# Idle products on TensorE in the state-space heads, and an early load of ScalarE's exponential table

## The chip, the cores and the metric

The kernel runs on one core of a Trainium2 chip. The metric is the device time of one execution in microseconds (us). The engines are TensorE (PE; its weight loads are PEld), VectorE (DVE), ScalarE (ACT), GpSimd (POOL) and SyncE (SP, which here issues DMAs).

## The reference

Two models run one after the other on 512 tokens of width 1024. The second has two layers, and the first layer mixes tokens with a state-space model (Mamba-2 style) of 16 heads, 64 values per head, a state of 128, in 4 chunks of 128 tokens. The part that matters:

```python
cb = jnp.einsum('bclgn,bcsgn->bclsg', cm, bm)
y_diag = jnp.einsum('bclsgr,bcsgrp->bclgrp', cb[..., None] * decay_ls, xdt)
chunk_states = jnp.einsum('bclgn,bclgrp->bcgrpn', bm, xdt * decay_to_end[..., None])
...
_, h_in = lax.scan(step, h0, (chunk_states, chunk_decay))      # h * decay + state, over the chunks
y_off = jnp.einsum('bclgn,bcgrpn->bclgrp', cm, h_in) * jnp.exp(a_cs)[..., None]
y = y_diag + y_off + xs * d_skip
```

`decay_ls` is the exponential of differences of a running sum `a_cs` of one number per head and token; `exp(a_cs)` weights the part that comes from earlier chunks.

## The kernel before

The whole program is one stream of instructions per engine, each executed in its written order, with semaphores between the engines. Almost all of TensorE's time is dense products of width 512 (`product`, L2776). The stretch that the change touches lies between two dense stages of the second model's first layer and takes about 71 us. In it TensorE does, in this order (`second_tensor`):

- **Chunk states** (`chunk_states`, L1931): for each of 3 chunks 2 products of 128x512 in f32. Each chunk waits for its scaled rows (`xde`), which DVE writes at L1642; those of the third chunk reuse the buffer of the first, so DVE waits there for the first chunk's product. DVE then runs the scan over the chunks (L1656 multiplies by the decay, L1660 adds the chunk's product out of PSUM) and raises `hin` at its end.
- **Spreads** (`spread`, L1938): for a head h one f32 product 128x512 that lays the running sum of that head over all partitions, into one of 4 PSUM banks (`aux`). The first four spreads wait for banks that L1660 of the scan gives back.
- **Pairs**: for j = 0 to 7, the spreads of heads 2j+4 and 2j+5 (none for j = 6 and 7), then a wait for DVE (`head_ce`, `head_g`), then the pair's 28 narrow f32 products (L1959, L1961), which multiply the values and the incoming states with the decay matrices of heads 2j and 2j+1 and write the PSUM tile `YD[j % 2]`.

For each head ACT takes the exponential of the spread (`CE`, L1366 or L1369) and of the differences (`GB`, L1367 or L1376); for even heads DVE forms the differences (`head_start`, L1675), for odd heads ACT does (L1372). DVE then multiplies both (`head_end`, L1680 and L1681). `CE` and `GB` have four buffers each, so `head_start(2j+2)` waits until pair j-1 is finished (`yd`). DVE executes `head_start(2j+2)` ahead of `head_end(2j+1)`, on which pair j waits. After `head_end(2j+1)` it adds the skip term to pair j-1 (`head_out`, L1665), which frees `YD` (`yd_taken`).

ACT holds one table of functions at a time. Ahead of the heads it used the table with Silu, so its first exponential (L1366) is preceded by a table load.

`keep_clock(bank, n)` (L2782) issues n f32 products of 128x512 from constants, whose result nobody reads. It is in use at several other places of the kernel.

Of the kernel before, what the change touches and what calls it, by code (L numbers as in the profile page):

```python
# [14 lines left out]
ACT = mybir.ActivationFunctionType  # L15
# [208 lines left out]
GROUP_NO = {g: i for i, g in enumerate(GROUPS)}  # L224
# [94 lines left out]
def build(nc, x_t, params, w_dense, p_t, w_moe, out_t, stop=None):  # L319
    ctx = ExitStack()  # L320
    with ctx:
# [34 lines left out]
        def flat(lo, n):  # L356
            return arena[:, lo:lo + n]
# [30 lines left out]
        def bank(name):  # L388
            return psA[:, AUX_NO[name] % 4, :]
# [4 lines left out]
        def ready(eng, name):  # L394

            eng.wait_ge(sem("aux_ready"), AUX_NO[name] + 1)

        def freed(name):

            return sem(f"aux_free{AUX_NO[name] % 4}")  # L400
# [5 lines left out]
        def group_freed(group):  # L406
            return sem(f"pair_free{GROUP_NO[group] % 2}")
# [835 lines left out]
        CE = [flat(27648 + 512 * i, 512) for i in range(4)]  # L1243
# [3 lines left out]
        ACST, DTT, DEC, DEE = (flat(32768 + 64 * i, 64) for i in range(4))  # L1247
        acst, dtt, dee = (t.rearrange("p (c h) -> p c h", c=4) for t in (ACST, DTT, DEE))
        dec = DEC.rearrange("p (h c) -> p h c", h=16)
        YD = [psD[:, GROUP_NO[("xbc", 5)] % 2, b, :] for b in range(2)]  # L1250
# [28 lines left out]
        def att(i):  # L1279

            n, j = i // 8, i % 8
            return n, j, P if n == 0 else 2 * P
# [31 lines left out]
        def second_act(act, step, root, ahead, x_hi):  # L1314
# [39 lines left out]
            for g in range(2):  # L1354
                n_ = ("stt", 0, g)
                ready(act, n_)
                act.activation(HIN[0][:, 512 * g:512 * g + 512], bank(n_), ACT.Copy).then_inc(freed(n_), 1)
            for h in range(16):
                n_ = ("acs", h)
                ready(act, n_)  # L1360
                if h >= 4:
                    act.wait_ge(sem("yd"), h // 2 - 1)

                if h % 2 == 0:
                    act.wait_ge(sem("seg"), h // 2 + 1)
                    act.activation(CE[h % 4], bank(n_), ACT.Exp).then_inc(freed(n_), 1)  # L1366
                    act.activation(GB[h % 4], GB[h % 4], ACT.Exp).then_inc(sem("seg_exp"), 1)  # L1367
                else:
                    act.activation(CE[h % 4], bank(n_), ACT.Exp)  # L1369
                    for c in range(4):  # L1370
                        cs = slice(P * c, P * c + P)
                        ins = act.activation(GB[h % 4][:, cs], bank(n_)[:, cs], ACT.Relu, bias=acst[:, c, h:h + 1],  # L1372
                                             scale=-1.0)
                    ins.then_inc(freed(n_), 1)
                    act.wait_ge(freed(n_), AUX_NO[n_] // 4 + 1)
                    act.activation(GB[h % 4], GB[h % 4], ACT.Exp, scale=-1.0).then_inc(sem("seg_exp"), 1)  # L1376
                if h == 13:
                    ahead.leave(("z", 0))
# [46 lines left out]
            for layer in range(2):  # L1425
                if layer == 1:
# [4 lines left out]
                    for i in range(N_ATT + 4):  # L1431
                        if i < N_ATT:
                            n, j, w = att(i)
# [13 lines left out]
                        if 2 <= i < N_ATT + 2:  # L1447
                            k = i - 2
                            _, _, w = att(k)
                            n_ = ("pt", k)  # L1450
                            ready(act, n_)
                            if k >= 2:
                                ready(act, ("pv", k - 2))
                            act.activation(PTB[k % 2][:, 0:2 * w], bank(n_)[:, 0:2 * w], ACT.Copy)\
                               .then_inc(freed(n_), 1)
                        if 3 <= i < N_ATT + 3:
                            k = i - 3
                            n, j, _ = att(k)
# [426 lines left out]
                if i >= 1:  # L1885
                    norm(i - 1)

        def second_tensor(pe, aux, filled, dense, colsum, weights, product, tile_of, spread_stat):
            xr = tile_of(X0_P)
            for j in range(8):  # L1890
                dense(("sc_ch", j), xr, at="x0" if j == 0 else None)
# [4 lines left out]
            out = aux(("da_t",))  # L1896
# [10 lines left out]
            for c in range(4):  # L1907
                out = aux(("bct", c))
# [3 lines left out]
            for c in range(4):  # L1912
                for h in range(2):
                    out = aux(("xst", c, h))
# [3 lines left out]
            for g in range(2):  # L1918
                out = aux(("cb", g))
# [8 lines left out]
            def chunk_states(c):  # L1928
                pe.wait_ge(sem("xde"), c + 1)
                for g in range(2):  # L1930
                    filled(pe.matmul(aux(("stt", c, g)), BTOK[:, c, g, :], XDE[c % 2][:, 512 * g:512 * g + 512],  # L1931
                                     start=True, stop=True))

            for c in range(3):
                chunk_states(c)

            def spread(h):
                filled(pe.matmul(aux(("acs", h)), SELH[0:16, h, :], DT[7][0:16, :], start=True, stop=True))  # L1938

            for h in range(4):  # L1940
                spread(h)
            pe.wait_ge(sem("hin"), 1)
            for j in range(8):
                for h in (2 * j + 4, 2 * j + 5):
                    if h < 16:
                        spread(h)
                out = YD[j % 2]
                if j == 0:
                    pe.wait_ge(group_freed(("xbc", 5)), GROUP_NO[("xbc", 5)] // 2 + 1)
                elif j >= 2:  # L1950
                    pe.wait_ge(sem("yd_taken"), j - 1)
                pe.wait_ge(sem("head_ce"), 2 * j + 2)
                pe.wait_ge(sem("head_g"), 2 * j + 2)
                for o_ in range(2):
                    h = 2 * j + o_
                    for c in range(4):
                        cs = slice(P * c, P * c + P)
                        dst = out[HD * o_:HD * o_ + HD, cs]
                        mm = pe.matmul(dst, XDT[:, c, HD * h:HD * h + HD], GB[h % 4][:, cs], start=True, stop=(c == 0))  # L1959
                        if c > 0:  # L1960
                            mm = pe.matmul(dst, HIN[c - 1][:, HD * h:HD * h + HD], CE[h % 4][:, cs],  # L1961
                                           start=False, stop=True)
                mm.then_inc(sem("yd"), 1)
# [58 lines left out]
            for layer in range(2):  # L2022
                if layer == 1:
# [17 lines left out]
                    for i in range(N_ATT + 3):  # L2041
                        if i < N_ATT:
                            n, j, w_ = att(i)
                            k0 = P * n + P - w_
                            out = aux(("sc", i))[:, 0:2 * w_].rearrange("p (o s) -> p o s", o=2)
# [5 lines left out]
                        if 2 <= i < N_ATT + 2:  # L2051
                            k = i - 2
                            _, _, w_ = att(k)
                            out = aux(("pt", k))
                            pe.wait_ge(sem("probs"), k + 1)
                            for b in range(2 * w_ // P):
                                mm = pe.transpose(out[:, P * b:P * b + P], PB[k % 4][:, P * b:P * b + P], ident)
                            filled(mm)
                        if i >= 3:
                            k = i - 3  # L2060
                            n, j, w_ = att(k)
                            nb = w_ // P
                            out = aux(("pv", k))
# [37 lines left out]
        def _(sp_):  # L2101
# [4 lines left out]
            def load(i):  # L2106
                _, nk, nco, _ = PLAN[i]
                if i >= RAW:

                    if i - RAW in SPLIT_NO:  # L2110
                        sp_.wait_ge(sem("w_lo"), SPLIT_NO[i - RAW] + 1)
                    else:
                        sp_.wait_ge(sem("units_done"), i - RAW + 1)
                lo = (i % RAW) * UNIT
                sp_.dma_start(ring[:, lo:lo + nk * nco], w_dense[i, :, 0:nk * nco])\
                   .then_inc(sem(f"ring_full{i % RAW}"), 16)
# [98 lines left out]
        def _(act):  # L2215
# [168 lines left out]
            if stop == 2:  # L2384
                return
            second_act(act, step, root, ahead, x_hi)


# [363 lines left out]
        def _(pe):  # L2752
            done_aux = [0]

            def aux(name):

                n = done_aux[0]
                assert AUX[n] == name, (AUX[n], name)
                done_aux[0] += 1
                if n >= 4:  # L2760
                    pe.wait_ge(sem(f"aux_free{n % 4}"), n // 4)
                return psA[:, n % 4, :]
# [18 lines left out]
            def keep_clock(bank_, n):  # L2781

                for _ in range(n):
                    pe.matmul(bank_, ones, masks[:, 0:SEQ], start=True, stop=True)
# [134 lines left out]
            for o_ in range(2):  # L2919
                out = aux(("lp", o_))  # L2920
# [185 lines left out]
            moe_tensor(pe, aux, filled, dense, colsum, product, keep_clock, spread)  # L3106
            if stop == 2:
                return
            second_tensor(pe, aux, filled, dense, colsum, weights, product, tile_of, spread)

STOP = None

# [27 lines left out]
```

## Time and profile before

| what | value |
|---|---|
| time, median of 3 runs | 2662.4 us (2660.02 to 2664.61) |
| time of the profiled execution | 2666.41 us |
| its span | 2664.7 us |
| mean granted TensorE clock | 0.972 of full speed |
| busy: PE, DVE, ACT, POOL | 95%, 55%, 43%, 6% of the span |

The span is what the profiler recorded of one execution; all times inside the kernel below count from its start. The profiled execution took 4.0 us more than the median of the runs. An f32 product of 128x512 leaves two records on PE, and so two entries in a count such as x12. Records of PE overlap (a product is shown until its result is out), so the distance between the starts of consecutive records tells how long one occupies the engine.

### The profile page before, as it was taken

The page shows a single profiled execution, that of the slowest core. Times are in us where ns is not written, and L with a number is a line of the kernel's source. Part 1 is how long each engine was busy: PE and PEld are TensorE (multiplying, and loading weights), DVE is VectorE, ACT ScalarE, POOL GpSimd, SP SyncE. Part 2 cuts the span into 40 slices and gives each one's busy share as a digit, 9 for nine tenths or more (in the row PEclk, how much of TensorE's full clock was granted, in tenths as well). Part 3 has the DMA queues.
Part 4 walks back from the last instruction along what each step waited for, and adds up shares of the span by engine and source line. Part 5 has one row for each costly group of instructions (what it writes and reads, how often), then busy time and mean ns, then how long its engine had stood idle before and what let it go on. Part 6 is the DMA issues. An engine that isn't in the chain of part 4 may idle for free.

```text
span 2664.7 us, 29458 instructions
## 1 busy us (share of the span) xinstructions
PE 2531.5 (95%) x12112; PEld 1962.4 (74%) x12112; DVE 1477.3 (55%) x1654; ACT 1132.9 (43%) x1329; POOL 147.8 (6%) x168
## 2 busy tenths in 40 slices
PE   7989996999999998999989999999989999999998
PEld 4667864887888886877757768888778567888876
DVE  3675545788888886546565353333454844323334
ACT  3422223777877876322344242122252644212223
POOL 1000001101111100000000100000100010000010
PEclk8888998999999999999979999999999999999999
DMA  6123403899999996322202222232322012232120
GB/s 259 62 72 124 168 10 139 307 369 359 367 352 360 361 357 260 145 96 79 79 1 79 95 71 81 101 109 67 103 77 95 17 48 79 79 108 99 65 101 32
DMA packets 64567, 388.76 MB, mean 146 GB/s; under 512 B 13360, under 2 KB 13488, under 8 KB 22576
## 3 DMA queue, kind: packets, MB, share of 16 engines
q1 hardware_dynamic: 53712, 373.20, 38.3%
q0 software_dynamic: 9280, 8.42, 0.9%
q10 hardware_dynamic: 1440, 5.24, 0.5%
q8 instruction: 97, 1.59, 0.2%
q14 instruction: 38, 0.31, 0.0%
HBM read 391.00 MB, written 20.97 MB: 155 GB/s over the span
## 4 chain that ended last, share of the span: by engine, by line
PE 86%; DVE 6%; ACT 3%; DMA 3%; issue 2%; POOL 0%; SPq 0%; DVEq 0%; ACTq 0%; POOLq 0%
PE psD L2776 71%; DMA ring<-w_moe 1%; PE psA L2015 1%; DMA ring<-w_dense 1%; PE psA L1085 1%; DVE ring_r L2429 1%; PE psA L2849 1%; ACT ring_r L2232 1%; PE psD L1959 1%; PE psA L2976 1%; PE psA L2046 1%; PE psA L3050 1%; PE psA L3036 1%; PE psA L2829 1%; PE psD L1961 1%
## 5 line engine op out<-in xcount | busy, mean ns | idle before, releaser
L2776 PE MATMUL psD<-rounded,ring_r 128*128 128x512 f32 (+1 forms) x6168 | 1457.0, 398 | 16.4 <-DVE ring_r L2429 12.6
L2776 PEld LDWEIGHTS psD<-rounded,ring_r 128*128 128x128 f32 (+1 forms) x6168 | 1159.4, 188 | 314.7 <-issue 23.4
L2429 DVE TENSOR_TENSOR ring_r<-ring,ring_r 128x2048 fp32r<-128x2048 f32 (+3 forms) x143 | 307.1, 2147 | 236.8 <-ACT ring_r L2232 232.6
L2232 ACT ACTIVATE ring_r<-ring 128x2048 fp32r<-128x2048 f32 (+3 forms) x143 | 252.0, 1762 | 390.8 <-PE psD L2776 370.7
L2776 PE MATMUL psD<-ring_r,rounded 128*128 128x512 f32 (+1 forms) x1728 | 410.5, 394 | 5.2 <-DVE rounded L976 2.9
L2776 PEld LDWEIGHTS psD<-ring_r,rounded 128*128 128x128 f32 x1728 | 319.0, 190 | 85.2 <-issue 7.3
L966 DVE TENSOR_TENSOR ring_r<-ring,ring_r 128x2048 fp32r<-128x2048 f32 x128 | 293.2, 2291 | 44.3 <-ACT ring_r L764 41.9
L764 ACT ACTIVATE ring_r<-ring 128x2048 fp32r<-128x2048 f32 x128 | 245.2, 1917 | 53.5 <-PE psD L2776 29.7
L2776 PE MATMUL psD<-rounded,rounded 128*128 128x512 f32 x768 | 191.8, 399 | 0.0
L1792 DVE TENSOR_TENSOR arena<-arena,psD 128x512 f32<-128x512 f32 x44 | 30.3, 688 | 254.7 <-ACT arena L1487 254.7
L2776 PEld LDWEIGHTS psD<-rounded,rounded 128*128 128x128 f32 x768 | 139.7, 188 | 27.1
L966 DVE TENSOR_TENSOR rounded<-ring,rounded 128x2048 fp32r<-128x2048 f32 x64 | 146.5, 2289 | 19.7 <-ACT rounded L764 19.6
L1487 ACT ACTIVATE arena<-psD 128x512 f32<-128x512 f32 x44 | 26.3, 598 | 307.5 <-PE psD L2776 307.4
L764 ACT ACTIVATE rounded<-ring 128x2048 fp32r<-128x2048 f32 x64 | 123.0, 1921 | 8.6 <-DMA ring<-w_moe 8.4
L2238 ACT ACTIVATE rounded<-arena 128x512 fp32r<-128x512 f32 x112 | 67.4, 627 | 59.4 <-DVE arena L1792 36.5
L683 POOL TENSOR_TENSOR arena<-arena 128x512 f32<-128x512 f32 x5 | 7.5, 1505 | 1354.6 <-DVE arena L1765 1280.5
L1765 DVE SCALAR_TENSOR_TENSOR arena<-arena,psD 128x512 f32<-128x512 f32 x40 | 27.5, 688 | 78.0 <-PE psD L2776 77.3
L677 POOL DMA_INDIRECT pair_rows<-arena,ints x32 | 33.9, 1059 | 510.7 <-ACT arena L780 477.4
L1797 DVE TENSOR_TENSOR rounded<-arena,rounded 128x512 fp32r<-128x512 f32 x44 | 30.5, 693 | 30.7 <-ACT rounded L2238 30.7
L971 DVE TENSOR_TENSOR rounded<-psA,rounded 128x1024 fp32r<-128x1024 f32 x32 | 39.2, 1225 | 14.2 <-ACT rounded L769 14.1
L686 POOL TENSOR_TENSOR arena<-arena 128x512 f32<-128x512 f32 x20 | 39.2, 1961 | 97.8 <-DVE arena L1765 92.3
L2849 PE MATMUL psA<-ring,par 128*32 128x256 f32 x384 | 28.7, 426 | 16.2 <-DMA ring<-w_dense 16.2
(423 smaller groups left out, 2094.5 us busy)
## 6 DMA issues: line engine op xcount, KB each, us to landing
ring<-w_moe SPq DMA_DIRECT2D x192, 1024.0 KB, 7.2
ring<-w_dense SPq DMA_DIRECT2D x134, 1024.0 KB, 4.8
ring<-w_dense SPq DMA_DIRECT2D x16, 768.0 KB, 4.1
ring<-w_dense SPq DMA_DIRECT2D x16, 640.0 KB, 3.9
arena<-x_t SPq DMA_DIRECT2D x1, 2048.0 KB, 7.9
token_rows<-arena ACTq DMA_DIRECT2D x4, 512.0 KB, 2.6
arena<-pair_rows SPq DMA_DIRECT2D x4, 512.0 KB, 7.7
arena<-pair_rows ACTq DMA_DIRECT2D x4, 512.0 KB, 8.1
```

The source lines that it names most:

```text
L677: return pool.indirect_dma_start(pair_rows, bass.IndirectOffsetOnAxis(ap=pair_i[:, e:e + 1], axis=0), buf, None, bounds_check=2 * SEQ - 1, ...
L686: step(pool.tensor_tensor(total, total, tiles[k], ALU.add))
L764: act.activation(expert_parts(E.place(j, PARTS))[0], slot_tile(slot), ACT.Copy).then_inc(sem("m_hi"), 1)
L966: dve.tensor_tensor(lo_, slot_tile(E.place(j, RAW)), hi, ALU.subtract).then_inc(sem("m_lo"), 1)
L971: dve.tensor_tensor(XEP[buf][1], x_banks, XEP[buf][0], ALU.subtract).then_inc(sem("xe_lo"), 1)
L1792: dve.tensor_tensor(TH[j % 2], SGT[j % 2], dbank(g)[:, 1, :], ALU.mult)\
L1797: dve.tensor_tensor(HID_P[1][:, j % HS, :], TH[j % 2], HID_P[0][:, j % HS, :], ALU.subtract).then_inc(sem("x_lo"), 1)
L2232: act.activation(parts_of(u, nk, nco)[0], ring_of(u, nk, nco), ACT.Copy).then_inc(sem("w_hi"), 1)
L2238: act.activation(dst, src, ACT.Identity if kw else ACT.Copy, **kw).then_inc(sem("x_hi"), 1)
L2429: dve.tensor_tensor(lo_, ring_of(u, nk, nco), hi, ALU.subtract).then_inc(sem("w_lo"), 1)
L2776: mm = pe.matmul(out, w[a], x[b], start=start and i == 0, stop=stop_ and i == 2)
L2849: mm = pe.matmul(out[32 * (k % 4):32 * (k % 4) + 32, 0:256], par[:, at + k:at + k + 32], w[:, k, :], start=(k < 4), stop=(k >= 4))
```

## The change

Three kinds of instructions are added, and one wait stands earlier; nothing is removed.

```diff
@@ second_act: ahead of the loop over the 16 heads
                 act.activation(HIN[0][:, 512 * g:512 * g + 512], bank(n_), ACT.Copy).then_inc(freed(n_), 1)
+            step(act.activation(CE[3][:, 0:1], DTT[:, 0:1], ACT.Exp))
             for h in range(16):
@@ second_tensor
+            pe.wait_ge(group_freed(("xbc", 5)), GROUP_NO[("xbc", 5)] // 2 + 1)
+            keep_clock(YD[0], 10)
             for c in range(3):
                 chunk_states(c)
...
             for h in range(4):
                 spread(h)
+            keep_clock(YD[0], 6)
             pe.wait_ge(sem("hin"), 1)
             for j in range(8):
                 for h in (2 * j + 4, 2 * j + 5):
                     if h < 16:
                         spread(h)
                 out = YD[j % 2]
-                if j == 0:
-                    pe.wait_ge(group_freed(("xbc", 5)), GROUP_NO[("xbc", 5)] // 2 + 1)
-                elif j >= 2:
+                if j >= 2:
                     pe.wait_ge(sem("yd_taken"), j - 1)
+                keep_clock(out, 5)
                 pe.wait_ge(sem("head_ce"), 2 * j + 2)
                 pe.wait_ge(sem("head_g"), 2 * j + 2)
```

On TensorE, from the chunk states to the second pair, the stream before was this (L1931 is the chunk states, L1938 the spreads, L1959 and L1961 the pairs):

```order
L1922 MATMUL psA<-arena 128x128 x8
L1931 MATMUL psA<-arena 128x512 x6
L1938 MATMUL psA<-arena 128x512 x6
L1959 MATMUL psD<-arena 64x128 x2
L1961 MATMUL psD<-arena 64x128
L1959 MATMUL psD<-arena 64x128
```

And it is now this, with the lines of the changed kernel (L1932, L1941, L1962 and L1964 are the same four, L2787 is `keep_clock`):

```order
L1923 MATMUL psA<-arena 128x128 x8
L2787 MATMUL psD<-masks 128x512 x10
L1932 MATMUL psA<-arena 128x512 x6
L1941 MATMUL psA<-arena 128x512 x4
L2787 MATMUL psD<-masks 128x512 x6
L1941 MATMUL psA<-arena 128x512 x2
L2787 MATMUL psD<-masks 128x512 x5
L1962 MATMUL psD<-arena 64x128 x2
L1964 MATMUL psD<-arena 64x128
```

Ten idle products stand ahead of the chunk states, six behind the first four spreads, and five between the spreads of heads 4 and 5 and pair 0. The same five stand ahead of each later pair; where a pair has no spreads, as the last one, they stand directly between two pairs:

```order
L1962 MATMUL psD<-arena 64x128
L1964 MATMUL psD<-arena 64x128
L2787 MATMUL psD<-masks 128x512 x5
L1962 MATMUL psD<-arena 64x128 x2
L1964 MATMUL psD<-arena 64x128
```

That makes 10 + 6 + 8 x 5 = 56 idle products more. On ACT, between the copies of the first states (L1357) and the first head, before:

```order
L1357 ACTIVATE arena<-psA 128x512 x2
L1366 ACT_TABLE_LOAD
L1366 ACTIVATE arena<-psA 128x512
L1367 ACTIVATE arena<-arena 128x512
```

And now:

```order
L1357 ACTIVATE arena<-psA 128x512 x2
L1358 ACT_TABLE_LOAD
L1358 ACTIVATE arena<-arena 128x1
L1367 ACTIVATE arena<-psA 128x512
L1368 ACTIVATE arena<-arena 128x512
```

The table load moved from the first head's exponential to the new exponential of a single column, which waits for nothing of the heads. DVE's stream and the DMAs are as before.

## Rows read from the trace of the kernel before

**Rows 1.** The page's busy times, one line: engines, busy us, share, instructions.

```profile
PE 2531.5 (95%) x12112; PEld 1962.4 (74%) x12112; DVE 1477.3 (55%) x1654; ACT 1132.9 (43%) x1329; POOL 147.8 (6%) x168
```

**Rows 2.** Windows of PE over the stretch: length, busy, granted clock, DMA share, GB/s.

```profile
1324.83:1396.10 71.27, 58.76 (x269) 0.76 0.00 1
1354.50:1361.80 7.30, 6.37 (x32) 0.77 0.00 0
1383.60:1389.30 5.70, 2.87 (x29) 1.00 0.00 0
1389.30:1396.10 6.80, 6.79 (x56) 0.75 0.01 2
```

**Rows 3.** Windows of PE, cut where the granted clock changes.

```profile
1324.80:1328.00 3.20, 0.06 (x2) 1.00 0.00 0
1328.50:1331.50 3.00, 3.00 (x5) 0.50 0.00 0
1332.00:1338.50 6.50, 6.17 (x15) 1.00 0.00 0
1339.00:1351.90 12.90, 11.03 (x35) 0.50 0.00 0
1352.20:1355.40 3.20, 2.52 (x12) 1.00 0.00 0
1355.70:1359.00 3.30, 3.30 (x21) 0.50 0.00 0
```

**Rows 4.** Timeline, chunk states to pair 0: start, us, engine, line, operation, idle before.

```profile
1327.97 7.09 PE L1931 MATMUL psA<-arena 128*128 128x512 f32 x12 [3.14 <-DVE arena L1642]
...
1331.48 1.23 DVE L1642 TENSOR_TENSOR arena<-arena 128x1024 f32<-128x1024 f32 x1 [2.62 <-PE psA L1931]
...
1332.63 0.68 DVE L1656 TENSOR_TENSOR arena<-arena 128x512 f32<-128x512 f32 x1
...
1337.68 0.69 DVE L1660 TENSOR_TENSOR arena<-arena,psA 128x512 f32<-128x512 f32 x1
...
1338.42 2.02 PE L1938 MATMUL psA<-arena 16*128 16x512 f32 x2 [0.33 <-DVE arena L1660]
...
1339.96 1.28 ACT L1366 ACT_TABLE_LOAD   x1 [7.88 <-DVE arena L1675]
1341.26 0.60 ACT L1366 ACTIVATE arena<-psA 128x512 f32<-128x512 f32 x1
...
1346.32 1.08 PE L1959 MATMUL psD<-arena 128*64 128x128 f32 x4 [0.31 <-DVE arena L1681]
```

**Rows 5.** Timeline of pairs 5 and 6, same columns.

```profile
1380.70 1.98 PE L1938 MATMUL psA<-arena 16*128 16x512 f32 x4
1380.89 1.36 DVE L1675 TENSOR_SCALAR arena<-psA,arena 128x128 f32<-128x128 f32 x4 [2.69 <-PE psD L1961]
...
1383.60 0.62 PE L1959 MATMUL psD<-arena 128*64 128x128 f32 x4 [0.92 <-DVE arena L1681]
...
1386.57 1.37 DVE L1675 TENSOR_SCALAR arena<-psA,arena 128x128 f32<-128x128 f32 x4 [1.26 <-PE psD L1961]
...
1389.29 0.69 PE L1959 MATMUL psD<-arena 128*64 128x128 f32 x4 [2.83 <-DVE arena L1681]
```

**Rows 6.** PE's waits from 1324 to 1397: us in total, times, longest.

```profile
PE psD L1959 <- DVE arena L1681: 7.5, 7, 2.8
PE psA L1931 <- DVE arena L1642: 3.1, 1, 3.1
```

**Rows 7.** Timeline: idle products that the kernel already has (two records per product).

```profile
1063.67 4.46 PE L2784 MATMUL psA<-masks 128*128 128x512 f32 x10
...
1396.93 2.84 PE L2784 MATMUL psD<-masks 128*128 128x512 f32 x6 [0.84 <-DVE arena L1665]
```

**Rows 8.** Timeline of PE alone, from the stretch's end on.

```profile
1399.82 45.03 PE L2776 MATMUL psD<-rounded,ring_r 128*128 128x512 f32 x192
1444.69 7.03 PE L2829 MATMUL psA<-arena,masks 128*128 128x512 f32 x16
1451.16 78.97 PE L2776 MATMUL psD<-rounded,ring_r 128*128 128x512 f32 x336
```

More of the change, by code:

```diff
@@ L1886, in attention, with second_tensor @@
                     norm(i - 1)
-        def second_tensor(pe, aux, filled, dense, colsum, weights, product, tile_of, spread_stat):
+        def second_tensor(pe, aux, filled, dense, colsum, weights, product, tile_of, spread_stat, keep_clock):
             xr = tile_of(X0_P)
@@ L3108, in _ @@
                 return
-            second_tensor(pe, aux, filled, dense, colsum, weights, product, tile_of, spread)
+            second_tensor(pe, aux, filled, dense, colsum, weights, product, tile_of, spread, keep_clock)
 STOP = None
```

## The prediction

> **What bounds the kernel now.** I read the page first: PE is busy 95% of the span [rows 1], so whatever is added to its stream must find a hole there. The windows show that the touched stretch is not like the rest: of 71.3 us PE is busy 58.8, and the granted clock averages 0.76, which means that it runs for about half of the time at 1.2 GHz instead of 2.4 [rows 2]. So there are 12.5 us of idle time and some lost clock to be had. Windows cut at the changes of the clock show when it falls: after PE has been idle for 3 us ahead of the chunk states, again after the first spreads, and in the middle of a pair; each short fall lasts some 3.3 us [rows 3].
>
> The timeline then shows the loop over the pairs [rows 5]. PE issues the two spreads of pair 5 from 1380.70 (1.98 us with the tail of the last record), and pair 5 itself starts at 1383.60, 0.92 us after PE ran out of work, released by DVE's L1681. DVE could start its own work for the next pair (L1675) only at 1380.89, when the pair before was done, and starts the next at 1386.57, when pair 5 is done. So the loop is a ring of two parts: a pair on PE, 1386.57 - 1383.60 = 2.97 us at the full clock, and then 1389.29 - 1386.57 = 2.72 us of DVE and ACT, of which PE fills 1.7 us with spreads where there are any. The table of waits says the same: the pairs waited 7.5 us in 7 waits for L1681, and the chunk states 3.1 us for L1642 [rows 6]. From 1346.32 to 1389.29 six pairs took 42.97 us [rows 4, 5], 7.16 us each, against 2.97 + 2.72 = 5.69 at a full clock: the slow clock costs 1.47 us a pair, the idle time about 1 us.
>
> Behind the stretch PE runs dense products without a gap for well over 100 us [rows 8], so nothing there gives back what the stretch loses, and nothing there was waiting for it to end early.
>
> **What one idle product costs.** Ten records, five products, took 4.46 us [rows 7]. The last record ends some 0.59 us after its start, so the other nine stand 0.43 us apart, and one product holds PE for 0.86 us at the full clock. At half the clock it is double, 1.72: the four records of the chunk states from 1327.97 to 1331.48 are two products of the same shape in 3.5 us [rows 4]. The engine executes in order, so none of this overlaps with the pair behind it. All 56 products cost 56 x 0.86 = 48.2 us of PE. The hole they stand in is 12.5 us, and a perfect clock could return less than half of the time spent at 1.2 GHz. That alone says that the change is too large for its place; the new timeline gives the amount.
>
> **The new timeline, step by step**, with everything at the full clock at first.
>
> - The chunk states. PE is done with the products before them at 1324.85. Ten idle products, 8.6 us, end at 1333.45, where before there was a wait until 1327.97; the clock should stay up, since the idle time that stood ahead of its fall is filled [rows 3]. Six products of chunk states take 5.16 us, to 1338.6.
> - The scan. DVE's third block of scaled rows waits for the first chunk's product, which is ready 1.72 us plus about 0.25 after 1333.45, at 1335.45, instead of 1331.48 [rows 4]. The whole chain of DVE behind it moves by 3.97 us. Its last L1660 started at 1337.68 and now starts at 1341.65 and ends near 1342.4.
> - The first spreads. They wait for banks that this chain frees; the fourth starts at 1342.4 and ends at 1343.25. Six idle products, 5.16 us, end at 1348.4.
> - The clock, once. Before, spreads held apart by DVE's bank returns were followed by a fall of the clock (6.50 us at 1.00, then 0.50) [rows 3]. That phase comes back unchanged in kind, so I take one fall of 3.4 us, the length that the short falls have, through dense work: + 1.7 us, to 1350.1.
> - Pair 0. Two spreads (1.72) and five idle products (4.3) end at 1356.1. ACT and DVE are ready long before: their L1366 started 2.9 us after the scan (with the table load in between) and pair 0 5.06 us after that [rows 4]; with the scan ending at 1342.4 this is 1349 even before anything is gained on ACT. Pair 0 ends at 1356.1 + 2.97 = 1359.1.
> - The table load. It leaves the path between DVE's L1675 and the first exponential, which is worth 1.28 us [rows 4], but that path now ends 7 us ahead of PE. I cost it at nothing. If the idle products were not there it would be worth its 1.28. The single-column exponential costs a fraction of the 0.60 us that a full one takes, in a place where ACT waited 7.88 us [rows 4].
> - Pairs 1 to 5. Spreads start 0.19 us ahead of DVE's L1675 [rows 5], take 1.72, then 4.3 of idle products, then 2.97 of the pair: 8.8 us, with 0.05 for the semaphores 8.85. DVE and ACT need only 2.72 of it behind a pair, so they drop out of the bound. Five pairs: 44.25 us, to 1403.4.
> - Pairs 6 and 7 have no spreads: 4.3 + 2.97 - 0.19 = 7.1 us each, to 1417.6. Pair 7 hurts most: before, it followed pair 6 without any wait, and both took 6.8 us together [rows 2].
> - The end. The next product of PE waited for L1665 of the last pair, some 0.8 us. It started at 1396.93 [rows 7] and now starts at 1418.4: **21.5 us later**.
>
> Against the profiled execution's own span this gives 2664.7 + 21.5 = 2686.2 us and 2687.9 us for its time; against the median of 2662.4, from which that execution stands 4.0 us off, **2683.9 us**. The same by budget: 48.2 of products, less the 12.5 idle, less 14 for the pairs and chunk states that run at the full clock, leaves 21.7.
>
> Of the clock the Trainium skill (TensorE: Matmul & The Clock Gate, "Why this matters for your kernels") says that it falls when long idle gaps stand between bursts of products. Here it fell behind spreads with only sub-microsecond gaps, and within a pair that came after 0.9 us of idle time, so the trace does not bear the rule out as a condition. By the page the fall behind the first spreads would not return, and the sum would be 1.7 us less: 2682.2.
>
> **The rivals.**
>
> - *The clock does not hold.* The pairs are narrow products and the spreads use 16 of the rows, so it may be that neither counts as much activity, and the clock still falls once a pair, for 3.3 us as in [rows 3]. Each fall in a stretch without idle time costs 1.7 us. Seven falls: + 12, so 2696. For it speaks that the clock fell in a pair after spreads that filled most of the time before. Against it: half of every new period consists of full-size products, and such products, back to back, keep the clock at 1.00 elsewhere. That would be "the change does not do what it says". Chance 0.11.
> - *Faster.* If the idle products fitted into the waits, the gain would be: six pairs at 5.69 instead of 7.16, 8.8 us; pairs 6 and 7, 1.0; the table load, 1.28; the first chunk's two products at the full clock, 1.7. Together 12.8 us, 2649.6. The mechanism is real, its size is the question: behind a pair PE has 0.19 + 2.72 = 2.91 us, less 1.72 for spreads, so 1.19 us are free, which is 1.4 products. Each further one adds 0.86 to the pair. It pays up to (1.19 + 1.47) / 0.86 = 3.1 products a pair; the change has 5, plus 16 in front. It could only win if a product took under 0.53 us here, and no row has one of this shape and type at less than 0.86. Chance 0.03. The skill's page ScalarE: Activation LUTs ("What ACT_TABLE_LOAD costs") gives 2.66 us for a switch with its drain, by which this rival would end at 2648.2; here only the 1.28 us of the load stand between L1675 and the exponential.
> - *No change that can be told* (a measurement of this kernel tells 0.2%, 5.3 us, from none). This needs 16 us of the 21.5 to be returned, for instance by dense stages that become shorter since ACT and DVE got ahead in splitting weights. But the splits stand at fixed places of their streams and PE does not wait for them behind the stretch [rows 8]. Chance 0.03.
> - *Slower by less*, 2669 to 2679: products overlap in part with the spreads' tails, or the profiled stretch was worse than that of a usual run. Chance 0.08.
>
> **How the numbers follow.** The forecast, 2684 with 2679 to 2689 of its own (with or without the one fall, 0.1 us either way a pair, 2 us of spread between runs), has 0.75. To leave out no more than 2 in 10 I widen it upward by the lesser half of the first rival: **2678 to 2692**. Slower by over 0.2%: 0.75 + 0.11 + 0.08 = 0.94; within 0.03; faster 0.03.
>
> **What would show the steps.** In the new trace idle products should fill 8.6 us ahead of the chunk states; the starts of the pairs should stand 8.85 us apart for pairs 1 to 5 and 7.1 behind; PE's wait for L1681 should be gone and DVE should wait 3 us more a pair for PE; the clock of the stretch should be near 1.00 except for one fall of 3.4 us near 1342 to 1346; the table load should stand near 1335; the stretch should be 93 us long instead of 71.3. A stretch at a mean clock of 0.8 would mean the first rival. I am wrong altogether if an idle product occupies PE for clearly less than 0.86 us, or if a dense stage behind gets shorter.

## The result, and the profile after

The changed kernel takes 2690.1 us in the median of 4 runs (2683.8 to 2692.7), against 2663.5 for before. The ratio is 1.0097, with a 95% interval of 1.0083 to 1.011: slower by about 26 us. The forecast was 2684 with 2678 to 2692.

The profiled execution of the changed kernel is the fastest of the four, 2683.8 us with a span of 2682.0. At least part of what it is ahead by has nothing to do with the change: the stretch began 6.5 us earlier in it than in the profile of before. The page's busy times, against [rows 1], show 34 us more of PE, with the 112 records of the 56 products, and next to nothing else:

```profile
PE 2565.3 (96%) x12224; PEld 1966.0 (73%) x12224; DVE 1476.8 (55%) x1654; ACT 1133.5 (42%) x1330; POOL 149.9 (6%) x168
```

Therefore I compare from here on the **stretch** itself, from the start of the products ahead of the chunk states (L1922, 16 records; one line further down where the early table load is in) to the start of the idle products that end it. In the kernel before it starts here:

```profile
1322.78 2.05 PE L1922 MATMUL psA<-arena 128*128 128x128 f32 x16
```

and ends at 1396.93 [rows 7], 74.15 us.

The timeline of the changed kernel, the stretch from its front to its end (start, us, engine, line, operation, idle before):

```profile
1316.30 2.05 PE L1923 MATMUL psA<-arena 128*128 128x128 f32 x16
1318.19 8.75 PE L2787 MATMUL psD<-masks 128*128 128x512 f32 x20
...
1326.77 5.31 PE L1932 MATMUL psA<-arena 128*128 128x512 f32 x12
...
1328.69 1.23 DVE L1643 TENSOR_TENSOR arena<-arena 128x1024 f32<-128x1024 f32 x1 [6.31 <-PE psA L1932]
...
1329.31 1.28 ACT L1358 ACT_TABLE_LOAD   x1
...
1335.64 2.07 PE L1941 MATMUL psA<-arena 16*128 16x512 f32 x2 [0.33 <-DVE arena L1661]
...
1337.21 0.60 ACT L1367 ACTIVATE arena<-psA 128x512 f32<-128x512 f32 x1 [6.41 <-DVE arena L1676]
...
1337.64 7.77 PE L2787 MATMUL psD<-masks 128*128 128x512 f32 x12
...
1345.34 1.98 PE L1941 MATMUL psA<-arena 16*128 16x512 f32 x4
...
1416.19 2.84 PE L2787 MATMUL psD<-masks 128*128 128x512 f32 x6 [0.84 <-DVE arena L1666]
```

The stretch is 1416.19 - 1316.30 = 99.89 us, 25.7 longer. That is the whole of the loss: the span grew by only 17.3 us, since the stretch began 6.5 us earlier and the program behind it took 2.0 us less. None of those 2.0 us lies in the dense products directly behind the stretch, whose two runs took 45.05 and 78.96 us against 45.03 and 78.97 [rows 8]. The ten products in front run from 1318.19 to 1326.77, 8.6 us. One round of the loop over the pairs, against [rows 5]:

```profile
1354.56 1.98 PE L1941 MATMUL psA<-arena 16*128 16x512 f32 x4
1354.74 1.36 DVE L1676 TENSOR_SCALAR arena<-psA,arena 128x128 f32<-128x128 f32 x4 [11.27 <-PE psD L1964]
...
1356.47 4.56 PE L2787 MATMUL psD<-masks 128*128 128x512 f32 x10
...
1360.96 0.65 PE L1962 MATMUL psD<-arena 128*64 128x128 f32 x4
...
1363.78 1.98 PE L1941 MATMUL psA<-arena 16*128 16x512 f32 x4
```

The spreads take 1.91 us with what follows them, the five idle products 4.49, the pair 2.82: a period of 9.22 us. No entry of PE shows a wait; DVE's last product for this pair (L1682 of its odd head, at 1356.62) is done at 1357.30, 3.7 us before the pair starts. The waits say the same, for DVE and PE, against [rows 6]:

```profile
DVE arena L1676 <- PE psD L1964: 35.2, 6, 11.3
PE psD L2787 <- DVE arena L1666: 0.8, 1, 0.8
PE psA L1941 <- DVE arena L1661: 0.5, 2, 0.3
```

PE no longer waits for DVE ahead of any pair (L1681, now L1682, is missing from its waits); DVE waits for PE instead, 35.2 us in 6 waits where it was 16.9 before. And the clock, in windows of 1.6 us around its only fall (length, busy, granted clock), against [rows 3]:

```profile
1334.80:1336.40 1.60, 1.27 (x3) 0.74 0.00 0
1336.40:1338.00 1.60, 1.60 (x3) 0.50 0.00 0
...
1341.20:1342.80 1.60, 1.60 (x4) 0.62 0.00 0
1342.80:1344.40 1.60, 1.60 (x6) 1.00 0.00 0
```

From the shares of the two mixed windows the fall lasts from 1335.6 to 1342.4, 6.8 us. In the 46 windows from 1342.8 on, up to 1416, the clock is 1.00 throughout. So the idle products did what they are for, and cost far more than that is worth.

### The profile page after: what moved, and what is told of

It reads as the page before. It is cut to its first block, busy times and chain, and to the rows that moved or that the text cites. A ratio compares the mean times of both kernels' runs of the same rounds, so it can differ in the third digit from the quotient of the medians.

```text
span 2682.0 us, 29683 instructions
## 1 busy us (share of the span) xinstructions
PE 2565.3 (96%) x12224; PEld 1966.0 (73%) x12224; DVE 1476.8 (55%) x1654; ACT 1133.5 (42%) x1330; POOL 149.9 (6%) x168
## 4 chain that ended last, share of the span: by engine, by line
PE 87%; DVE 5%; ACT 3%; DMA 2%; issue 2%; POOL 0%; SPq 0%; DVEq 0%; ACTq 0%; POOLq 0%
PE psD L2779 70%; PE psD L2787 3%; DMA ring<-w_moe 1%; PE psA L2018 1%; DMA ring<-w_dense 1%; DVE ring_r L2432 1%; PE psA L1085 1%; PE psA L2852 1%; ACT ring_r L2235 1%; PE psA L2049 1%; PE psA L2979 1%; PE psA L3053 1%; PE psA L2832 1%; PE psA L3039 1%; PE psA L2787 1%
## 5 line engine op out<-in xcount | busy, mean ns | idle before, releaser
L2787 PE MATMUL psD<-masks 128*128 128x512 f32 x176 | 87.2, 646 | 1.7 <-DVE arena L1666 0.8
L683 POOL TENSOR_TENSOR arena<-arena 128x512 f32<-128x512 f32 x5 | 7.5, 1506 | 1381.3 <-DVE arena L1766 1307.2
L2787 PEld LDWEIGHTS psD<-masks 128*128 128x128 f32 x176 | 34.4, 203 | 46.3 <-issue 44.6
```

## The experiments

All eleven ran as variants of the kernel before or of the changed one. In all of them the wait for `xbc` stands ahead of the chunk states, as in the changed kernel; PE's idle time there still ended with DVE's L1642. The stretch comes from each one's profile, the ratio from the timed runs against before.

| run | what | stretch, us | against 74.15 | ratio (95%) |
|---|---|---|---|---|
| changed kernel | 10 + 6 in front, 5 a pair, table | 99.89 | +25.7 | 1.0097 (1.0083 to 1.011) |
| e1 | table load alone | 71.82 | -2.3 | 0.9994 (0.9981 to 1.0006) |
| e2 | 5 a pair alone | 95.11 | +21.0 | 1.008 (1.0054 to 1.0107) |
| e3 | 1 a pair alone | 69.42 | -4.7 | 0.9984 (0.997 to 0.9999) |
| e4 | 3 a pair alone | 79.84 | +5.7 | 1.0022 (1.0009 to 1.0036) |
| e5 | 3 ahead of the chunk states alone | 72.42 | -1.7 | 1.0 (0.9987 to 1.0013) |
| e6 | changed kernel, idle products of 64 columns | 95.61 | +21.5 | 1.0082 (1.0056 to 1.0108) |
| e7 | DVE's order alone | 67.50 | -6.7 | 0.997 (0.9957 to 0.9984) |
| e8 | e7 with table and 3 in front | 66.08 | -8.1 | 0.9972 (0.9959 to 0.9984) |
| e9 | heads of a pair alternate | 70.23 | -3.9 | 0.9987 (0.9974 to 1.0) |
| e10 | sized: table, 3 in front, 1 a pair | 65.97 | -8.2 | 0.9967 (0.9955 to 0.9979) |
| e11 | e10 and e9 | 58.77 | -15.4 | 0.9953 (0.9938 to 0.9968) |

**e1, the table load alone.**

```diff
+            step(act.activation(CE[3][:, 0:1], DTT[:, 0:1], ACT.Exp))
```

> Kernel before with the early single-column exponential alone, no idle products. My theory (DVE and ACT are on the path where no idle products cover it, the load costs 1.28 us between L1675 and the first exponential): the stretch from the start of the products ahead of the chunk states (L1922) to the idle products at its end gets 1.3 us shorter than the 74.1 us of before, the time 0.05% less, too little to be told from the runs alone. Rival (a switch of tables also costs a drain, 2.66 us by the page ScalarE: Activation LUTs of the Trainium skill): the stretch gets 2.7 us shorter.

The place in question, DVE's differences for head 0 and the exponential behind them, in the timeline of e1:

```profile
1337.03 1.36 DVE L1676 TENSOR_SCALAR arena<-psA,arena 128x128 f32<-128x128 f32 x4 [0.15 <-DVE arena L1661]
...
1338.51 0.60 ACT L1367 ACTIVATE arena<-psA 128x512 f32<-128x512 f32 x1 [6.41 <-DVE arena L1676]
```

From start to start 1.48 us, where before it took from L1675 at 1338.52 to L1366 at 1341.26 [rows 4], 2.74. The load was worth 1.26 us there, its own duration, and no drain comes back with it. The stretch gained 2.3; the other microsecond lies ahead of that place, in the chunk states: from L1923 to DVE's third L1643 it took 7.67 us against 8.70 before, with the same instructions on PE and DVE. The granted clock in windows of e1 shows why:

```profile
1328.50:1329.00 0.50, 0.50 (x3) 0.84 0.00 0
1329.00:1329.50 0.50, 0.50 (x2) 0.50 0.00 0
```

The chunk states began at 1327.51 and the clock fell at 1328.8, 1.3 us later; before, it fell 0.3 us after they began. So the first chunk's products ran mostly at the full clock here. Nothing in the change does that. A single profile's stretch is good to no better than one or two microseconds for that reason (more on this at e5).

**e2, e3, e4, the number of idle products a pair.** Each is the kernel before with one line (and the wait for `xbc` moved up with it), n = 5, 1 and 3:

```diff
+                keep_clock(out, n)
                 pe.wait_ge(sem("head_ce"), 2 * j + 2)
```

> Kernel before with five idle products ahead of each pair, neither the ten nor the six in front and no early table load. My theory (PE executes in order, 40 products of 0.86 us, pairs 1 to 5 at a period of 9.2 us, pairs 6 and 7 at 7.3): +20.6 us, most of the whole change. Rival (the cost lies in the 16 products in front): at most +8 us.

> One idle product ahead of each pair instead of five, nothing else. My theory of the hole: spreads 1.72, a product 0.86 and two changeovers of 0.19 us fill the 2.91 us that PE has behind a pair. If that holds the clock, pairs 1 to 5 come every 5.8 us and the time falls by about 5 us. Rival (one product does not hold the clock, the pairs still lose a half-clock phase each): period 7.2 us, time +1 to +2 us from pairs 0 and 7.

> Three idle products ahead of each pair, nothing else. My theory (in order, each product over the hole adds 0.86 us; the clock holds): period 7.5 us for pairs 1 to 5 against 7.16 before, 5.6 us each for pairs 6 and 7 which took 6.8 us together, pair 0 some 4 us later: +8 us in all. Rival (the number beyond the hole does not matter because the regained clock pays for it, the break-even of 3.1 products holds for the stretch as a whole): within 2 us of the time before.

With five the stretch gets 21.0 us longer, as forecast (20.6): the loop is most of the loss. With one, the timeline of e3 shows a round:

```profile
1356.65 1.12 PE L2784 MATMUL psD<-masks 128*128 128x512 f32 x2
...
1360.52 1.98 PE L1939 MATMUL psA<-arena 16*128 16x512 f32 x4
1362.43 1.12 PE L2784 MATMUL psD<-masks 128*128 128x512 f32 x2
```

and its windows the clock:

```profile
1350.00:1355.00 5.00, 5.00 (x30) 0.60 0.00 0
1355.00:1360.00 5.00, 5.00 (x31) 1.00 0.00 0
```

From the first round with spreads behind pair 0 (1354.74) on, the period is 5.78 us against 7.16 and the clock stays at 1.00, and the stretch is 4.7 us shorter. One product a round is enough here, and the rival that it would not hold the clock is out. With three, the idle products start at:

```profile
1356.09 2.84 PE L2784 MATMUL psD<-masks 128*128 128x512 f32 x6
1363.59 2.84 PE L2784 MATMUL psD<-masks 128*128 128x512 f32 x6
...
1391.70 2.84 PE L2784 MATMUL psD<-masks 128*128 128x512 f32 x6
1397.39 2.84 PE L2784 MATMUL psD<-masks 128*128 128x512 f32 x6
```

7.50 us a round, two products of 0.86 more than e3, and 5.7 for the rounds without spreads. The loss of 5.7 us is somewhat under the 8 expected. Pair 0 did start 3.8 us later, counted from the front of the stretch, as I had put it; but it ran at the full clock, in 2.8 us instead of 5.3, so that only 1.3 us of this were left at the spreads behind it. Pairs 1 to 5 cost 2.8 us (four periods of 7.50 against 7.26, and pair 5, which before had the full clock already, 1.8), and pairs 6 and 7 with the end 1.6. The periods of the three runs, 5.78, 7.50 and 9.22 us, lie two products of 0.86 us apart each time: a product beyond the hole costs its own time.

**e5, three in front.**

```diff
+            keep_clock(YD[0], 3)
             for c in range(3):
                 chunk_states(c)
```

> Kernel before with three idle products ahead of the chunk states, which fit into the 3.1 us in which PE waits there. My theory: the clock does not fall at 1328, the first chunk's two products take 1.7 us less, DVE's scan starts 1.7 us earlier and the stretch from L1922 to the idle products at its end (74.1 us before) gets 1.7 us shorter. Rival (the fall only moves to a later place of the same path): no gain, 0 to 2 us in the other direction.

The stretch is 1.7 us shorter, as expected, and the timed runs can't tell it (ratio 1.0). The profiles can, in the part that is concerned: from the front of the stretch to DVE's third L1642 it took 7.02 us in e5, and the same 7.02 in e8, e10 and e11, the other runs with three products there. In the seven profiles without products in front it took 8.70 (before), 7.67 (e1), 8.87 (e2), 8.78 (e3), 7.94 (e4), 7.19 (e7) and 8.71 (e9), with the same instructions. So in these profiles three products made this part steady, and what they gained is 0.2 to 1.9 us, by when the clock fell without them.

**e6, another shape of the idle products, in the changed kernel.**

```diff
-                keep_clock(out, 5)
+                for _ in range(5):
+                    pe.matmul(out[0:HD], ones[:, 0:HD], masks[:, 0:SEQ], start=True, stop=True)
```

> The changed kernel, with the five idle products ahead of each pair made with 64 columns of weights, the shape of the pair's own products, instead of 128. They move as many rows and should take the same 0.86 us each. Theory A (the 0.19 us that PE loses between the idle products and the pair comes from the change of shape): it vanishes, the period falls from 9.22 to 9.03 us, the stretch by 1.5 us from 99.9. Theory B (the weight load behind the semaphore wait is exposed): nothing changes. Time within 0.1% of the changed kernel in either case; the profile decides.

The period fell from 9.22 to 9.02, as theory A said: from the first idle product to the pair it is 4.34 us in place of 4.49, so most of the gap behind the idle products comes from the change of shape and not from the wait. But the stretch lost 4.3 us and not 1.5. The six rounds with spreads give 1.2 of it. Another 1.6 us have nothing to do with the shape. They lie behind the first spreads, where e6 and the changed kernel have the same instructions:

```profile
1345.37 6.94 PE L2788 MATMUL psD<-masks 128*128 128x512 f32 x12
...
1352.24 1.98 PE L1941 MATMUL psA<-arena 16*128 16x512 f32 x4
```

From the end of the chunk states (1340.57) to these spreads it took 11.7 us in e6 and 13.3 in the changed kernel, since the clock was at 0.50 for 3.4 us here and for 6.8 there. The last 1.5 us came at the two rounds without spreads (timeline of e6):

```profile
1405.85 0.64 PE L1955 MATMUL psD<-masks 128*64 128x512 f32 x1
...
1406.06 0.38 PE L1965 MATMUL psD<-arena 128*64 128x128 f32 x2
1406.33 4.03 PE L1955 MATMUL psD<-masks 128*64 128x512 f32 x9
1410.19 0.60 PE L1963 MATMUL psD<-arena 128*64 128x128 f32 x4
```

The first idle product (L1955, lower 64 partitions of `YD`) starts at 1405.85, while products of the pair (L1963, L1965, by then on the upper 64) go on to 1406.4. Products on different halves of the columns run at the same time. These rounds take 6.58 us instead of 7.31.

**e7, DVE's order.**

```diff
             for h in range(17):
-                if h < 16 and h % 2 == 0:
-                    head_start(h)
                 if h >= 1:
                     head_end(h - 1)
+                if h < 16 and h % 2 == 0:
+                    head_start(h)
+                if h >= 4 and h % 2 == 0:
+                    head_out(h // 2 - 2)
```

(`head_out` moves out of `head_end`, so that it still stands behind `head_start`.)

> No idle products and no early table load. Kernel before with another order on DVE: head_end(2j+1), on which pair j waits, stands ahead of head_start(2j+2), which waits for pair j-1. My theory (a pair waits for DVE only because DVE is stuck behind the wait for the pair before): the pairs follow each other at PE's own pace, 1.9 us of spreads and 2.8 of the pair, 4.7 to 5 us instead of 7.16, and a PE that is never idle keeps its clock: 13 us less, 0.5%. Rival (the low clock is the bound, the pairs stay at 1.2 GHz for some other reason): period about 7, no gain.

It is 6.7 us shorter and not 13. A round in its timeline, and ahead of it the chunk states:

```profile
1330.36 5.39 PE L1931 MATMUL psA<-arena 128*128 128x512 f32 x12 [3.14 <-DVE arena L1642]
...
1370.70 1.36 DVE L1675 TENSOR_SCALAR arena<-psA,arena 128x128 f32<-128x128 f32 x4
...
1372.18 0.60 ACT L1366 ACTIVATE arena<-psA 128x512 f32<-128x512 f32 x1 [2.72 <-DVE arena L1675]
...
1374.84 0.63 ACT L1376 ACTIVATE arena<-arena 128x512 f32<-128x512 f32 x1
1375.50 0.69 DVE L1680 TENSOR_TENSOR arena<-arena 128x512 f32<-128x512 f32 x1 [0.88 <-ACT arena L1376]
1376.11 0.68 DVE L1681 TENSOR_TENSOR arena<-arena 128x512 f32<-128x512 f32 x1
1376.71 1.36 DVE L1675 TENSOR_SCALAR arena<-psA,arena 128x128 f32<-128x128 f32 x4
1376.94 0.62 PE L1958 MATMUL psD<-arena 128*64 128x128 f32 x4 [0.90 <-DVE arena L1681]
```

The wait for the pair before is gone, and another ring has taken its place, without PE: DVE's L1675, ACT's five steps to L1376, DVE's L1680 and L1681, and again L1675, 6.01 us. ACT waits 2.72 us in each round for L1675. It waited for it before too, about 4.0 us a round, but there L1675 itself waited for PE; with the new order ACT's own five steps stand in the ring. My account left this ring out. Nor did the clock hold: PE still waited 0.9 us in some rounds, and it fell once more inside the loop (0.66 in 1365 to 1370). And 1.5 us of the 6.7 are luck: after the same 3.14 us without work the clock did not fall at the chunk states, which took 5.3 us instead of 7.0, so DVE's third L1642 came at 7.19 us and not at 8.70. The order itself is worth about 5.

**e8, the same with table and front.**

```diff
+            step(act.activation(CE[3][:, 0:1], DTT[:, 0:1], ACT.Exp))
...
+            keep_clock(YD[0], 3)
```

> e7 with the early table load and three idle products ahead of the chunk states. My theory: the three gains lie one behind the other on one path and add up, 13 + 1.3 + 1.7 = 16 us less than before, 0.6%. Rival (with the order on DVE changed PE bounds the stretch and the other two gain nothing): the same as e7.

1.4 us shorter than e7, half of what I had added up; the timed runs show no difference. The missing half is the front: in e7 the clock had stayed up there without it, so the three products had only 7.19 - 7.02 = 0.2 us left to give, and the rest is the table load's 1.26.

**e9, the heads of a pair alternate.**

```diff
-                for o_ in range(2):
-                    h = 2 * j + o_
-                    for c in range(4):
+                for c in range(4):
+                    for o_ in range(2):
+                        h = 2 * j + o_
```

(The products of the incoming states alternate in the same way.)

> Kernel before, no idle products; only the order inside a pair is changed: the products of its two heads, which write the lower and the upper 64 partitions of YD, alternate instead of standing one head behind the other. Theory from the run with 64 columns of weights (its idle products on the lower half started while the pair's products on the upper half were still running): products on different halves run at the same time, the 28 products of a pair take some 1.5 us instead of 2.8 at the full clock and the pairs come 1.3 us (full clock) to 2.6 us (half clock) sooner each: 10 to 15 us less. Rival (that overlap was only at the border between two kinds of products, and the 56 records stay 0.055 us apart): period 7.2 us, no change.

Windows of PE in e9, the second one at the spreads of pair 1 and the pair itself:

```profile
1326.00:1391.00 65.00, 57.01 (x242) 0.58 0.00 0
1350.00:1356.00 6.00, 6.00 (x28) 0.50 0.00 0
```

The pairs did get shorter, but the clock fell and stayed at 0.50 through the whole loop: pair 0 took 3.2 us from its start to the next spreads (against 5.3 before, also wholly at half the clock), but the spreads of a round now took 3.7 us in place of 1.9, and the period was 6.9 us. The rival is out, since the halves overlap; but the expected 10 to 15 us shrank to 3.9, since I had reckoned with the clock of before.

**e10, the change sized to its holes, and e11, with alternating heads.**

```diff
+            step(act.activation(CE[3][:, 0:1], DTT[:, 0:1], ACT.Exp))
...
+            keep_clock(YD[0], 3)
...
+                if j < 7:
+                    keep_clock(out, 1)
```

> The change made to fit its holes: early table load, three idle products ahead of the chunk states, none behind the first spreads, one ahead of pairs 0 to 6, none ahead of pair 7. Theory (the gains measured one by one lie on one path and add up: 4.7 for one product a pair, 1.05 more for the one taken from pair 7, 1.3 for the table load, 1.7 for the front): the stretch falls from 74.1 to about 65.4 us, the time by 8 to 9 us. Rival (they regain the same half-clock phases and do not add up): 68 to 69 us, like one product a pair alone.

> e10 with the two heads of a pair alternating as in e9. If both theories hold, a pair costs about 1.5 us on PE and 2.9 behind it, a period near 4.4 us at the full clock, and the stretch is 10 us shorter than in e10, about 55 us, the time 18 us less than before. Rival (PE is now idle for longer, or the halves share the array less well at the full clock, and the clock falls in spite of the idle product): 60 us or more.

e10 came out at 65.97 us for 65.4 expected: the gains of single parts add up, within what the clock adds or takes from one profile to the next. It beats the kernel before by 0.33%, with ten idle products in all instead of 56. A round of e11:

```profile
1341.16 1.98 PE L1941 MATMUL psA<-arena 16*128 16x512 f32 x4
...
1343.07 1.13 PE L2789 MATMUL psD<-masks 128*128 128x512 f32 x2
...
1344.12 0.66 PE L1961 MATMUL psD<-arena 128*64 128x128 f32 x8
...
1345.80 1.98 PE L1941 MATMUL psA<-arena 16*128 16x512 f32 x4
```

```profile
1345.00:1350.00 5.00, 5.00 (x44) 1.00 0.02 3
...
1365.00:1370.00 5.00, 3.22 (x30) 0.76 0.01 3
```

The pair takes 1.68 us instead of 2.82, the period is 4.64 us, and the clock holds at 1.00 through the rounds of pairs 1 to 5; it falls again at the last pairs, which have no spreads. The stretch is 58.8 us, between theory (55) and rival (60), and the kernel the fastest of all, 0.47% below before. Here the idle product matters most: without it the same order of products gained 3.9 us, with it (and the table and front of e10) 15.4. No run has the table and the front without the product, so how the difference divides is not shown; e10 had gained 8.2 with all three and the old order.

## Why the prediction was right

The mechanism was right, and so was the greater part of the sum; that the number fell into the range is in part luck. The prediction gave its own sum 2679 to 2689, and the measured 2690.1 lies above that. It is inside 2692 only by the widening for the first rival, a clock that does not hold, and that rival did not come about.

- **The bound.** "Whatever is added to its stream must find a hole there": confirmed by e3, e4 and e2: -4.7, +5.7 and +21.0 us for 1, 3 and 5 products a pair. One fits the hole and returns the clock; each further one costs its time.
- **The price of a product**, 0.86 us: confirmed, ten in 8.6 us.
- **The scan**, moved by the wait for the first chunk's product: confirmed. It started 1.92 us after the chunk states did; I had put 2.0.
- **The table load at nothing.** In the changed kernel ACT's exponential at 1337.21 came straight behind DVE's differences, and PE worked through the fourth spread and six idle products meanwhile, until 1345.34, so the load is covered; uncovered it is worth 1.26 (e1), as the row of 1.28 said. The Trainium skill's 2.66 us with drain (ScalarE: Activation LUTs, "What ACT_TABLE_LOAD costs") is not what comes back here. (The prediction had ACT and DVE ready at 1349 "even before anything is gained on ACT"; its terms, 1342.4 + 2.9 + 5.06, give 1350.4, and 1349 with the load gained. Nothing hangs on it: DVE was done with pair 0's two heads at 1342.1, 9.6 us ahead of the pair.)
- **The rival of a clock that does not hold** is out: 1.00 in each window of the loop. The fall behind the first spreads did come back, with PE idle for 0.33 us at most ahead of it, so the sum without it (2682.2) is out too.
- **Dense stages behind**, which might have become shorter, did not: 45.05 and 78.96 us.
- **Where the sum was off**: 21.5 us were forecast for the stretch, it is 25.7. Two terms carry this. First, "one fall of 3.4 us": there was one fall, at the place I said, but it lasted 6.8 us, and PE worked through nearly all of it, also with the fourth spread (2.0 us instead of 0.86); from the end of the chunk states to the spreads of heads 4 and 5 it took 13.3 us instead of 11.5, 1.8 more. The length was taken from short falls in the loop; [rows 3] also had one of 13 us at the spreads themselves. The code does not fix this length: in e6, with the same instructions up to there, the fall lasted 3.4 us and this part took 11.7, as forecast. So the term could have come out right or wrong by chance. Second, "8.85 us" a round: it was 9.22. I let one kind of product follow another without loss, and PE loses about 0.19 us each time the shape changes: six times from spreads to idle products and eight times to a pair, 14 x 0.19 = 2.7 us. Together 4.5.
- **The break-even of 3.1 products a pair** was too high. With two changeovers it is (1.19 - 0.38 + 1.47) / 0.86 = 2.7 for a pair with spreads, and pair 7 has no hole at all; e4 with three lost 5.7 us.
- **The faster rival's mechanism** was real, as its own paragraph said, and worth 8.2 us in e10 out of the 12.8 put down for an ideal fit.

## What to carry to other kernels

Idle products are worth having only as long as they end before the work they stand ahead of is ready; measure that hole, subtract what already fills it and about 0.2 us for each change of shape, and divide by the product's own time. Here one product in each round of 6 us held the clock, and five cost 21 us. And a change that shortens real work can lose its gain to the clock (e9); then one idle product beside it can return it (e11). Before a difference of one or two microseconds between two profiles is put down to a change, compare when the clock fell in each (e1, e6, e7).

## What the runs showed of the hardware that was not expected

- Products of 64 columns on different halves of the columns run at the same time: alternating, a pair's 28 products took 1.68 us instead of 2.82. The Trainium skill (TensorE: Matmul & The Clock Gate, "Why this matters for your kernels") states this for small column counts; the traces of e6, e9 and e11 agree, for f32 too.
- The same work done in parallel halves no longer held the clock: 0.50 through the whole loop of e9, although by its records PE was busy all the time from 1350 to 1380.
- Changing from spreads (16 rows) to full products, or from these to products of 64 columns, costs PE about 0.19 us each. With 64 columns on both sides of the second border (e6) most of it was gone, 0.15 of 0.19. What makes the first border cost as much was not tried.
- The same 3.14 us without work on PE ahead of the chunk states had a fall of the clock 0.3 us into them (before), 1.3 us into them (e1), or none until the spreads 8 us later (e7). So one trace doesn't tell what an idle time of this length costs.
- Although the code ahead of it is the same in all these kernels, the stretch started between 1315.8 and 1325.2 us into the span. This difference is as large as most effects studied here. Part of it goes with the clock: ahead of the stretch the traces have 75 us at half the clock in the changed kernel (start 1316.3) and 79 in e8 (1315.8), but 89 in the kernel before (1322.8) and 92 in e7 (1325.2). It does not in every run (e5: 92 us, 1319.9), and the cause stays open.
